# Joint attentions of a streaming encoder step: the next tile's transposes ahead of the prompt scores in seven steps of eight

## The chip, the cores and the metric

The kernel runs on one core of a Trainium2 chip. The metric is the device time of one execution in microseconds. Its engines are named as in the profile: PE (TensorE, matrix products; PEld is its weight load), DVE (VectorE), ACT (ScalarE), POOL (GpSimd) and SP (SyncE, which issues the DMAs). Before the change three runs took 3592.12, 3593.35 and 3600.36 us, median 3593.35.

## The reference

One inference step of a two-layer encoder trunk, in float32. 1024 new frames of one stream (the prompt) and 16 new frames of each of 8 running streams (the decode part, with a cache of 2048 earlier frames) go through a layer with window attention (A) and differential attention (B), and a layer with forgetting attention (C), each followed by a dense SwiGLU. B and C are the two joint attentions of this case. Cut to what they compute:

```python
# B: pairs of heads share values; chunk mask
scores = einsum('bthed,bshed->bhets', q2, k2) * SCALE
p = softmax(where(chunk_mask, scores, NEG_INF))
attn = p[:, :, 0] - lam * p[:, :, 1]
out = einsum('bhts,bshd->bthd', attn, v)
# C: 16 heads; scores get the summed log forget values; causal mask
scores = einsum('bthd,bshd->bhts', q, k) * SCALE + cq - ck
p = softmax(where(kpos <= qpos, scores, NEG_INF))
out = einsum('bhts,bshd->bthd', p, v)
```

Both are computed for the prompt over itself and for the decode frames over cache and new frames. Besides the two outputs of the trunk the kernel returns the new keys, values and forget values.

## The kernel before, in words

The program is a row of stages: projection for A and B, window attention of the prompt and of the decode frames, joint attention B (names with jb_), merge and feed forward, projection for C, joint attention C (jc_), merge and feed forward. B and C run the same function, `joint_attention`, which computes the prompt's attention and the decode attention together, interleaved by hand in one instruction list for each engine. There is no scheduler: what is written first on an engine runs first, and engines meet in semaphores that count up.

The work goes in units u, 8 in jb and 16 in jc. A unit is one prompt head (64 columns of query and key) plus a share of the decode attention of one stream, of which u's scores are made at the unit's end and its softmax and values in the next unit, u+1. The last pass of the loop finishes the last decode part. A unit has 8 steps s, one for each tile of 128 prompt queries; n = 8u+s counts the steps. A tile t attends to t+1 tiles of keys, and the tiles are taken in the order 3, 4, 2, 5, 1, 6, 0, 7.

For one tile n the prompt's work goes through the engines like this:

- `score(n)` on PE (L1489 to L1491): scores of the tile, t+1 tiles of 128 keys wide, in split float32 (two products, 3 to 5 matmuls with the mask). Even tiles write the PSUM buffer scores_a, odd ones scores_b, so score(n) waits for exponential n-2 (`exp_done`).
- DVE takes the negated row maximum (L1774, neg_top).
- ACT takes the exponential into probs (L1694). It waits for the maximum, and until turn(n-2) has read the same probs buffer.
- DVE takes the reciprocal of the row sums (L1783, inv).
- `turn(n)` on PE (L1500): t+1 transposes of 128 x 128 of the probabilities, in groups of four tiles into a ring of two PSUM slots (turned). It waits for exponential n, and in `ring_slot` until ACT has copied out what stood in the slot two groups ago.
- ACT copies each group to probs_t in SBUF (L1659), which frees the slot.
- `attend(k)` on PE (L1517), once for each pair of tiles 2k and 2k+1, in the odd step behind: values times probabilities, into PSUM pv. It waits for the copies, for ACT's copy of the pair before (o_copied) and for both outputs of the pair before (out_done).
- ACT copies pv to o_turn (L1703); `turn_back(k)` on PE (L1529 in jb, L1532 in jc) turns it back, into the other half of the same PSUM bank; DVE scales it with inv into out (L1809; L1805 in every other head of jb, where it adds to the first head's).

On DVE one step n issues, in this order: at odd n the output of pair (n-3)/2, then the maximum of tile n+3, half of the key transposes of the decode part (L1828) that belong to the step, other decode work, the reciprocal of tile n, and the other half of the key transposes.

On ACT a step n issues exponential n+2, at even n the copy of pv, and then copy_prompt(n+1), with the decode part's copies (L1714, L1680) and exponentials (L1727) between them.

On PE a step n issues score(n+3), turn(n+1), and then what the step's number asks for: score_new (L1569 to L1575), turn_probs (L1589), attend at odd n, attend_sample (L1607), score_keys at s=7 (L1544, L1552), turn_back at even n, turn_output (L1615). PE's list starts with score(0), score(1), score(2), turn(0).

The ring of two slots is shared: the groups of turn, the decode scores of the new frames (one slot, s=5) and half of the decode key scores (two slots, s=7) take slots in turn. After s=7 the first turn of the next unit therefore waits for ACT's copies of the key scores.

SP loads keys and values of cache and prompt into double or single buffers and stores the outputs; its list and POOL's set-up are not touched.

Of the kernel before, what the change touches and what calls it, by code (L numbers as in the profile page):

```python
# [1151 lines left out]
def joint_attention(nc, name, groups, planes, k_first, v, v_cols, dv, q_sample, q_first, k_cache, v_cache, k_new, v_new,  # L1152
# [51 lines left out]
    def tile_at(n):  # L1204
        return order[n % S]
# [27 lines left out]
    with Stage(nc, name) as st:  # L1233
# [55 lines left out]
        def scores_of(n):  # L1289
            return scores_a[:] if n % 2 == 0 else scores_b[:]  # L1290
# [171 lines left out]
        def _(pe):  # L1462
            def ring_slot(key):
                r = seq[key]
                if r >= ring:
                    old = key_at[r - ring]
                    pe.wait_ge(emptied_sem[engine_of[old]], count[old])
                return turned[:, r % ring]
# [7 lines left out]
            def score(n):  # L1476
                if n >= steps:
                    return
                h, t = n // S, tile_at(n)
                e = h % 2  # L1480
                if n % S == 0:
                    pe.wait_ge(qk_loaded[e], 16 * n_qk_loads * (h // 2 + 1))
                if n >= 2:
                    pe.wait_ge(exp_done, n - 1)
                size = (t + 1) * P
                dst, query = scores_of(n), slice(t * P, (t + 1) * P)
                for a in range(0, size, 512):
                    b = min(a + 512, size)
                    pe.matmul(dst[:, a:b], q_hi[:, e, query], k_both[:, e, a:b], start=True, stop=False)  # L1489
                    pe.matmul(dst[:, a:b], q_lo[:, e, query], k_hi[:, e, a:b], start=False, stop=(b < size))  # L1490
                pe.matmul(dst[:, size - P:size], ident_b[:], mask[:], start=False, stop=True).then_inc(scores_done, 1)  # L1491

            def turn(n):
                if n >= steps:
                    return
                pe.wait_ge(exp_done, n + 1)
                for g, (a, b) in enumerate(group_of_step[n % S]):
                    slot = ring_slot(("p", n, g))
                    for x in range(a, b):
                        last = pe.transpose(slot[:, (x - a) * P:(x - a + 1) * P], probs[:, n % 2, x * P:(x + 1) * P], ident[:])  # L1500
                    last.then_inc(turn_done, 1)

            def attend(k):
                if not 0 <= k < pairs_p:
                    return
                h, t = 2 * k // S, tile_at(2 * k)
                if k % S == 0:
                    pe.wait_ge(v_loaded[h // 2 % 2], 16 * (h // 4 + 1))
                wait_emptied([("p", n, g) for n in (2 * k, 2 * k + 1) for g in range(len(group_of_step[n % S]))])
                if k >= 1:  # L1510
                    pe.wait_ge(o_copied, k)
                    pe.wait_ge(out_done, 2 * k)
                first = 0 if diff else h % 2 * dv
                for x in range(tile_at(2 * k + 1) + 1):
                    part = 0 if diff else x % 2 * dv
                    e = 0 if x <= t else 1
                    last = pe.matmul(pv[part:part + dv, e * P:2 * P], vp[:, h // 2 % 2, x, first:first + dv],  # L1517
                                     probs_t[:, k % 2, x, e:2, :].rearrange("p e q -> p (e q)"),
                                     start=(x < P // dv), stop=(x > tile_at(2 * k + 1) - P // dv), skip_group_check=True)
                last.then_inc(pv_done, 1)  # L1520
# [37 lines left out]
            def score_new(u):  # L1558
                if u == 0:
                    pe.wait_ge(setup, 14)  # L1560
                    if not diff:
                        pe.wait_ge(later_loaded, 80)
                pe.wait_ge(ktn_done, u + 1)
                pe.wait_ge(q_done, 2 * (u + 1))
                if not diff:
                    pe.wait_ge(bias_loaded[u % 2], 80 * (u // 2 + 1))
                slot = ring_slot(("sn", u))
                if not diff:
                    pe.matmul(slot[:, 0:FRAMES], ident[:], later[:], start=True, stop=False, skip_group_check=True)  # L1569
                    pe.matmul(slot[:, 0:FRAMES], select[Q:2 * Q], bias[Q:2 * Q, u % 2, bank:], start=False, stop=False,  # L1570
                              skip_group_check=True, tile_position=(Q, 0))
                for step in range(4):
                    for c in range(4):
                        hb = 4 * c + step
                        last = pe.matmul(slot[Q * c:Q * c + Q, 0:FRAMES], q_blocks[Q:2 * Q, hb // 2, hb % 2],  # L1575
                                         ktn[:, Q * hb:Q * hb + FRAMES], start=(diff and step == 0), stop=(step == 3),
                                         skip_group_check=True, tile_position=(Q, Q * c))
                last.then_inc(turn_done, 1)

            def turn_probs(u, gi):  # L1580
                a, b = PG[gi]
                pe.wait_ge(s_exp_done, 2 * u + (1 if b <= per * 2 else 2))
                pe.wait_ge(s_copied, 2 * (u + 1))
                if gi >= 2:
                    pe.wait_ge(pt_copied, len(PG) * u + (1, 3, 4)[gi - 2])
                for t in range(a, b):
                    m = P if t < tiles - 1 else FRAMES
                    c = (t - a) * P
                    last = pe.transpose(s_ps[0:m, bank_of[gi], c:c + P], s_probs[:, t * P:t * P + m], ident[:])  # L1589
                last.then_inc(pt_done, 1)  # L1590

            def attend_sample(u, part):
                pe.wait_ge(pt_copied, len(PG) * u + (2, 4)[part])
                if part == 0:
                    pe.wait_ge(s_copied, 2 * (u + 1))
                else:
                    pe.wait_ge(vnew_loaded, 16 * (u + 1))
                for t in ((range(0, 2 * per), range(2 * per, tiles))[part]):
                    new = t == tiles - 1
                    m = FRAMES if new else P  # L1600
                    if new:
                        pe.wait_ge(pt_copied, len(PG) * (u + 1))
                    elif t % per == 0:
                        pe.wait_ge(vc_loaded[t // per], 16 * (u + 1))
                    for j in range(4):
                        values = vn[:, j * P:(j + 1) * P] if new else vc[:, t // per, t % per, j * P:(j + 1) * P]
                        last = pe.matmul(o_ps[32 * j:32 * j + 32, :], s_probs_t[0:m, t, 32 * j:32 * j + 32], values,  # L1607
                                         start=(t == 0), stop=new, skip_group_check=True)
                if part == 1:
                    last.then_inc(s_pv_done, 1)  # L1610
# [11 lines left out]
            for u in range(U + 1):  # L1622
                for s in range(S):
                    n = S * u + s
                    score(n + 3)
                    turn(n + 1)
                    if u < U and s == 5:
                        score_new(u)
                    if 1 <= u <= U and s == 5:
                        for gi in probs_at[s]:  # L1630
                            turn_probs(u - 1, gi)
                    if n % 2 == 1:
                        attend((n - 1) // 2)
                    if 1 <= u <= U and s == 3:
                        for gi in probs_at[s]:
                            turn_probs(u - 1, gi)
                    if 1 <= u <= U and s == 5:
                        turn_probs(u - 1, 4)
                        attend_sample(u - 1, 1)
                    if u < U and s == 7:  # L1640
                        score_keys(u)
                    if n % 2 == 0:
                        turn_back((n - 2) // 2)
                    if 1 <= u <= U and s == 4:
                        attend_sample(u - 1, 0)
                        turn_probs(u - 1, 2)
                    if 1 <= u <= U and s == 6:
                        turn_output(u - 1)
# [1225 lines left out]
```

## Time and profile before

| what | value |
|---|---|
| median of three runs | 3593.35 us |
| profiled execution | 3596.04 us, its span 3594.3 us, mean granted TensorE clock 0.966 |
| instructions in the profile | 62088 |
| PE busy | 3327.7 us, 93% of the span |
| PE weight load busy | 2908.6 us, 81% |
| DVE busy | 1598.0 us, 44% |
| ACT busy | 1124.3 us, 31% |
| POOL busy | 254.9 us, 7% |
| DMA | 493.16 MB, mean 137 GB/s |

The span is the time from the first to the last instruction of the program; the execution's own time has 1.7 us more around it. The busy shares are averages over stages of different kinds. The joint attentions are the stretches from about 416 to 702 us (jb) and from about 2063 to 2598 us (jc); the feed-forward stages fill most of the rest. A busy time of PE is not PE at its peak, because matmuls overlap and their ends are modelled. In the order of time, a row is a run of instructions of one line: its start, its length to the end of the last one, and in brackets the idle time before it and who ended it. Since matmuls overlap, the next row may start before the length has passed.

### The profile page before, as it was taken

The page shows a single profiled execution, that of the slowest core. Times are in us where ns is not written, and L with a number is a line of the kernel's source. Part 1 is how long each engine was busy: PE and PEld are TensorE (multiplying, and loading weights), DVE is VectorE, ACT ScalarE, POOL GpSimd, SP SyncE. Part 2 cuts the span into 40 slices and gives each one's busy share as a digit, 9 for nine tenths or more (in the row PEclk, how much of TensorE's full clock was granted, in tenths as well). Part 3 has the DMA queues.
Part 4 walks back from the last instruction along what each step waited for, and adds up shares of the span by engine and source line. Part 5 has one row for each costly group of instructions (what it writes and reads, how often), then busy time and mean ns, then how long its engine had stood idle before and what let it go on. Part 6 is the DMA issues. An engine that isn't in the chain of part 4 may idle for free. (4 is left out here: it accounts for less than half of the span.)

```text
span 3594.3 us, 62088 instructions
## 1 busy us (share of the span) xinstructions
PE 3327.7 (93%) x24520; PEld 2908.6 (81%) x24520; DVE 1598.0 (44%) x2913; ACT 1124.3 (31%) x2343; POOL 254.9 (7%) x338
## 2 busy tenths in 40 slices
PE   7997699798999999998799889999798999999997
PEld 7886477587999999997689866767577999999996
DVE  5427477463333333335331167777543333333334
ACT  4215355443212112112322155556433211121111
POOL 2310000032000000003000000000022000000003
PEclk9998799899999999999899999999999999999999
DMA  5436499533111111112554399999543111111112
GB/s 172 125 125 189 148 373 333 178 138 117 35 35 58 35 47 35 35 47 71 153 167 145 104 348 357 341 335 342 197 172 117 35 35 48 45 47 35 35 38 97
DMA packets 398381, 493.16 MB, mean 137 GB/s; under 512 B 68464, under 2 KB 250256, under 8 KB 398032
## 3 DMA queue, kind: packets, MB, share of 16 engines
q1 hardware_dynamic: 398176, 490.35, 41.2%
q8 instruction: 138, 2.26, 0.3%
q14 instruction: 67, 0.55, 0.0%
HBM read 407.10 MB, written 84.10 MB: 137 GB/s over the span
## 5 line engine op out<-in xcount | busy, mean ns | idle before, releaser
L2561 DVE TENSOR_TENSOR f_gated<-f_gated,f_up 128x384 f32<-128x384 f32 x132 | 73.1, 554 | 734.9 <-ACT f_gated L2491 734.9
L2585 DVE TENSOR_TENSOR f_y<-f_y,f_down 128x512 f32<-128x512 f32 x396 | 269.7, 687 | 229.4 <-PE f_down L2680 229.3
L2667 PE MATMUL f_gate<-m_ht_hi,f_w_hi 128*128 128x384 f32 x1056 | 355.0, 336 | 12.1 <-DVE f_w_lo L2612 12.1
L2667 PE MATMUL f_gate<-m_ht_lo,f_w_hi 128*128 128x384 f32 x1056 | 354.4, 336 | 0.0
L2667 PE MATMUL f_gate<-m_ht_hi,f_w_lo 128*128 128x384 f32 x1056 | 354.4, 336 | 0.0
L2667 PE MATMUL f_up<-m_ht_hi,f_w_lo 128*128 128x384 f32 x1056 | 352.7, 334 | 0.0
L2667 PE MATMUL f_up<-m_ht_hi,f_w_hi 128*128 128x384 f32 x1056 | 352.7, 334 | 0.0
L2667 PE MATMUL f_up<-m_ht_lo,f_w_hi 128*128 128x384 f32 x1056 | 352.7, 334 | 0.0
L2680 PE MATMUL f_down<-f_wo_hi,f_act_hi 128*128 128x512 f32 x792 | 313.4, 396 | 10.6 <-DVE f_y L2585 9.3
L2680 PE MATMUL f_down<-f_wo_hi,f_act_lo 128*128 128x512 f32 x792 | 309.9, 391 | 0.0
L2680 PE MATMUL f_down<-f_wo_lo,f_act_hi 128*128 128x512 f32 x792 | 309.6, 391 | 0.0
L2491 ACT ACTIVATE f_gated<-f_gate 128x384 f32<-128x384 f32 x132 | 65.0, 493 | 684.5 <-PE f_up L2667 684.3
L2667 PEld LDWEIGHTS f_gate<-m_ht_hi,f_w_hi 128*128 128x128 f32 x1056 | 199.5, 189 | 13.6 <-issue 12.8
L2667 PEld LDWEIGHTS f_gate<-m_ht_lo,f_w_hi 128*128 128x128 f32 x1056 | 199.5, 189 | 0.8
L2667 PEld LDWEIGHTS f_gate<-m_ht_hi,f_w_lo 128*128 128x128 f32 x1056 | 199.4, 189 | 0.0
L2667 PEld LDWEIGHTS f_up<-m_ht_hi,f_w_hi 128*128 128x128 f32 x1056 | 198.2, 188 | 0.0
L2667 PEld LDWEIGHTS f_up<-m_ht_lo,f_w_hi 128*128 128x128 f32 x1056 | 198.2, 188 | 0.0
L2667 PEld LDWEIGHTS f_up<-m_ht_hi,f_w_lo 128*128 128x128 f32 x1056 | 198.2, 188 | 0.0
L2680 PEld LDWEIGHTS f_down<-f_wo_hi,f_act_hi 128*128 128x128 f32 x792 | 149.5, 189 | 52.7 <-DVE f_y L2585 19.0
L1828 DVE STREAM_TRANSPOSE jc_kc<-jc_kc 128x512 f32<-128x512 f32 x256 | 180.8, 706 | 14.2
L2680 PEld LDWEIGHTS f_down<-f_wo_hi,f_act_lo 128*128 128x128 f32 x792 | 149.2, 188 | 31.8
L2680 PEld LDWEIGHTS f_down<-f_wo_lo,f_act_hi 128*128 128x128 f32 x792 | 149.5, 189 | 29.9
(404 smaller groups left out, 6756.6 us busy)
## 6 DMA issues: line engine op xcount, KB each, us to landing
jc_kc<-in_cache_c_k SPq DMA_DIRECT2D x64, 1024.0 KB, 11.1
jc_vc<-in_cache_c_v SPq DMA_DIRECT2D x64, 1024.0 KB, 10.3
jb_kc<-in_cache_b_k SPq DMA_DIRECT2D x32, 1024.0 KB, 11.7
jb_vc<-in_cache_b_v SPq DMA_DIRECT2D x32, 1024.0 KB, 8.6
m_raw<-in_w_ffn_in SPq DMA_DIRECT2D x44, 512.0 KB
f_raw<-in_w_ffn_in SPq DMA_DIRECT2D x44, 512.0 KB
f_raw_o<-in_w_ffn_out SPq DMA_DIRECT2D x22, 1024.0 KB, 6.2
m_raw<-x SPq DMA_DIRECT2D x18, 512.0 KB, 4.1
```

The source lines that it names most:

```text
L1828: dve.transpose(kc[:, u % 2, t, :], kc[:, u % 2, t + 1, :]).then_inc(kt_done, 1)
L2491: act.activation(silu[:, b], gate[:, q, 0:gw], ACT.Silu).then_inc(silu_done, 1)
L2561: dve.tensor_tensor(prod[:, b], silu[:, b], up[:, q, 0:gw], ALU.mult).then_inc(prod_done, 1)
L2585: dve.tensor_tensor(part, part, down[:, half, :], ALU.add).then_inc(added, 1)
L2667: last = pe.matmul(acc[:, q, 0:gw], a[:, s, k, u, :], b[:, k, token], start=(k == 0 and j == 0), stop=(k == KT - 1 and j == 2))
L2680: last = pe.matmul(down[:, half, :], a[:, s, t * P:(t + 1) * P], b[:, s, half * 512:(half + 1) * 512], start=(n == 0), stop=(n == 5))
```

## The change

In PE's list the order of the first two parts of a step is exchanged in the steps s=1 to s=7 of every unit: turn(n+1) stands first and score(n+3) second. In s=0 the order is the old one. No other list changes.

```diff
             for u in range(U + 1):
                 for s in range(S):
                     n = S * u + s
-                    score(n + 3)
+                    if s == 0:
+                        score(n + 3)
                     turn(n + 1)
+                    if s > 0:
+                        score(n + 3)
                     if u < U and s == 5:
                         score_new(u)
```

The first place is PE's list around s=2 and s=3 of a unit in jc: turn is L1500, score is L1489 to L1491, turn_back is L1532 and attend is L1517; x6 and x2 are the number of transposes.

```order
-L1500 MATMUL jc_turned<-jc_ident,jc_probs 128x128 x6
 L1532 MATMUL jc_pv<-jc_halves,jc_o_turn 128x64 x2
+L1500 MATMUL jc_turned<-jc_ident,jc_probs 128x128 x2
 L1489 MATMUL jc_scores_a<-jc_k_both,jc_q_hi 128x128
 L1490 MATMUL jc_scores_a<-jc_k_hi,jc_q_lo 128x128
 L1491 MATMUL jc_scores_a<-jc_mask,jc_ident_b 128x128
-L1500 MATMUL jc_turned<-jc_ident,jc_probs 128x128 x2
 L1517 MATMUL jc_pv<-jc_probs_t,jc_vp 64x256 x3
 L1517 MATMUL jc_pv<-jc_probs_t,jc_vp 64x128 x3
```

The two transposes of s=3 move from behind the step's score to in front of it, so the score now stands directly ahead of attend; the six of s=2 have left their place behind that step's score for one ahead of it.

The second place is PE's list around s=6 and s=7 of a unit in jc, with the same names; L1615 is turn_output.

```order
-L1500 MATMUL jc_turned<-jc_ident,jc_probs 128x128 x8
 L1532 MATMUL jc_pv<-jc_halves,jc_o_turn 128x64 x2
 L1615 MATMUL jc_s_ps<-jc_ident,jc_o_rows 128x128
+L1500 MATMUL jc_turned<-jc_ident,jc_probs 128x128 x4
 L1489 MATMUL jc_scores_a<-jc_k_both,jc_q_hi 128x384
 L1490 MATMUL jc_scores_a<-jc_k_hi,jc_q_lo 128x384
 L1491 MATMUL jc_scores_a<-jc_mask,jc_ident_b 128x128
-L1500 MATMUL jc_turned<-jc_ident,jc_probs 128x128 x4
 L1517 MATMUL jc_pv<-jc_probs_t,jc_vp 64x256
 L1517 MATMUL jc_pv<-jc_probs_t,jc_vp 64x128 x7
```

The eight transposes of s=6 no longer stand between that step's score and turn_back, and the four of s=7 stand ahead of the score instead of ahead of attend.

## Rows read from the trace of the kernel before

**Rows 1.** Busy time by window: jb and jc without their first units.
```profile
470.00:680.00 210.00, 201.09 (x2953) 158.82 (x2967) 156.74 (x369) 121.72 (x299) 0.00 (x0) 1.00 0.85 301
2110.00:2570.00 460.00, 438.47 (x6729) 322.10 (x6725) 335.44 (x757) 274.50 (x674) 0.00 (x0) 1.00 0.95 332
```

**Rows 2.** PE's waits in jc, 2110 to 2570: total us, times, longest.
```profile
PE jc_pv L1532 <- ACT jc_o_turn L1703: 9.0, 15, 0.6
...
PE jc_pv L1517 <- DVE jc_out L1809: 3.6, 15, 0.3
```

**Rows 3.** PE in order of time, one jc unit from 2265: start, length, what.
```profile
2267.54 0.36 PE L1489 MATMUL jc_scores_a<-jc_k_both,jc_q_hi 128*128 128x256 f32 x1
...
2267.93 0.49 PE L1500 MATMUL jc_turned<-jc_ident,jc_probs 128*128 128x128 f32 x3
...
2270.65 0.82 PE L1500 MATMUL jc_turned<-jc_ident,jc_probs 128*128 128x128 f32 x6
2271.31 0.56 PE L1532 MATMUL jc_pv<-jc_halves,jc_o_turn 128*128 128x64 f32 x4
...
2272.74 1.27 PE L1517 MATMUL jc_pv<-jc_probs_t,jc_vp 128*64 128x256 f32 x12 [0.23 <-DVE jc_out L1809]
...
2275.88 0.93 PE L1500 MATMUL jc_turned<-jc_ident,jc_probs 128*128 128x128 f32 x7
2277.41 0.66 PE L1532 MATMUL jc_pv<-jc_halves,jc_o_turn 128*128 128x64 f32 x4 [0.60 <-ACT jc_o_turn L1703]
...
2287.04 1.04 PE L1500 MATMUL jc_turned<-jc_ident,jc_probs 128*128 128x128 f32 x8
2287.92 0.56 PE L1532 MATMUL jc_pv<-jc_halves,jc_o_turn 128*128 128x64 f32 x4
...
2289.39 1.30 PE L1517 MATMUL jc_pv<-jc_probs_t,jc_vp 128*64 128x256 f32 x16
```

**Rows 4.** DVE in order of time, the same jc unit.
```profile
2271.08 1.07 DVE L1774 TENSOR_REDUCE jc_neg_top<-jc_scores_b 128x1 f32<-128x896 f32 x1
...
2272.14 0.46 DVE L1809 TENSOR_SCALAR jc_out<-jc_pv,jc_inv 128x64 f32<-128x64 f32 x2
...
2287.24 0.82 DVE L1774 TENSOR_REDUCE jc_neg_top<-jc_scores_b 128x1 f32<-128x640 f32 x1 [0.52 <-PE jc_scores_b L1491]
...
2288.67 0.44 DVE L1809 TENSOR_SCALAR jc_out<-jc_pv,jc_inv 128x64 f32<-128x64 f32 x2
```

**Rows 5.** ACT in order of time, the same jc unit.
```profile
2266.99 0.77 ACT L1659 ACTIVATE jc_probs_t<-jc_turned 128x512 f32<-128x512 f32 x2 [0.43 <-PE jc_turned L1500]
```

**Rows 6.** PE in order of time, one jb unit from 557.
```profile
559.99 0.52 PE L1500 MATMUL jb_turned<-jb_ident,jb_probs 128*128 128x128 f32 x3 [0.20 <-ACT jb_probs_t L1659]
...
565.35 2.20 PE L1517 MATMUL jb_pv<-jb_probs_t,jb_vp 128*128 128x256 f32 x12 [0.16 <-DVE jb_out L1809]
...
569.26 0.93 PE L1500 MATMUL jb_turned<-jb_ident,jb_probs 128*128 128x128 f32 x7
...
570.46 1.96 PE L1607 MATMUL jb_s_ps<-jb_vc,jb_s_probs_t 128*32 128x128 f32 x64
...
574.46 2.14 PE L1517 MATMUL jb_pv<-jb_probs_t,jb_vp 128*128 128x256 f32 x14
...
582.02 2.23 PE L1517 MATMUL jb_pv<-jb_probs_t,jb_vp 128*128 128x256 f32 x16
```

**Rows 7.** ACT in order of time, the same jb unit.
```profile
559.25 0.77 ACT L1659 ACTIVATE jb_probs_t<-jb_turned 128x512 f32<-128x512 f32 x2 [0.41 <-PE jb_turned L1500]
```

**Rows 8.** DVE in order of time, the same jb unit.
```profile
563.53 1.09 DVE L1774 TENSOR_REDUCE jb_neg_top<-jb_scores_b 128x1 f32<-128x896 f32 x1 [0.33 <-PE jb_scores_b L1491]
...
564.61 0.59 DVE L1809 TENSOR_SCALAR jb_out<-jb_pv,jb_inv 128x128 f32<-128x128 f32 x2
...
573.23 0.57 DVE L1809 TENSOR_SCALAR jb_out<-jb_pv,jb_inv 128x128 f32<-128x128 f32 x2
...
581.31 0.57 DVE L1809 TENSOR_SCALAR jb_out<-jb_pv,jb_inv 128x128 f32<-128x128 f32 x2
```

## The prediction

> **What bounds the kernel now.** The first view is the busy time of the engines over the two joint attention stages, without their first units [rows 1]. In jb PE is busy 201.1 of 210 us, in jc 438.5 of 460, at a granted clock of 1.00 (the higher of its two levels, 2.4 GHz) in both. DVE and ACT are near or under three quarters, the DMA engines at 0.85 and 0.95. PE's own instructions fill these stages, so a change of PE's order alone can win or lose only the time in which PE waits. The second view, PE's waits in jc, shows how little that is [rows 2]: 15 waits of 0.6 us, one a unit, for the ACT copy that turn_back needs, 9.0 us together, and 15 of at most 0.3 us for the output that attend waits for, 3.6 us. The third view is the order of time on PE, DVE and ACT in one steady unit of each stage, for the waits and for what stands just short of becoming one [rows 3 to 8].
>
> I call the steps of a unit s0 to s7. Step s holds score(s+3) and turn(s+1). The order table gives the turns of s1 to s7 the sizes 3, 6, 2, 7, 1, 8, 4 tiles, one transpose a tile. Eight transposes take 0.88 us of PE (2287.04 to 2287.92), so 0.11 each; six take 0.66 [rows 3].
>
> **The change part by part.** No instruction is added or removed, and none changes its engine or shape. DVE, ACT and the DMA queues keep their order. In s1 to s7 PE's transposes go in front of three to five score matmuls. Score(n+3) overwrites the scores that exponential n+1 reads, and turn(n+1) reads what that exponential writes, so both wait for the same event and that wait merely changes its holder. Three things do change.
>
> First, turn has a second wait, for a ring slot that ACT must have copied out. Until now the score stood in front of it and covered it. In jb turn of s1 waits 0.20 us for that copy even so, and starts 0.74 us after the copies begin (559.25 to 559.99) [rows 6, 7]. In front, it holds up the score, and everything behind it in PE's queue: 0.39 us of score (2267.54 to 2267.93 in jc, the same shape) now follow the wait instead of passing under it. jb: +0.39 in s1. In jc the copies begin at 2266.99 [rows 5]; 0.74 later is 2267.73, and PE arrives at 2267.54: +0.19. For the other turns I take no such wait: the copies they need stand in ACT's list a step earlier, and in s3, where one could be late, attend waits longer for its output (below). Bound 0.2 each, as in jb's s1.
>
> Second, each score ends later by the transposes put in front of it, and behind a score hangs a chain: DVE takes the row maximum, then a reciprocal, in s6 a key transpose, then scales the previous pair's output, and attend of the next odd step waits for that output, since both use one bank. attend starts 0.14 us after the output's end (2272.14+0.46 to 2272.74) [rows 3, 4], the maximum 0.20 us after PE's last score (2287.24 against 2287.04).
> - jc, s3: score(5) was done at 2270.65, the maximum could have begun at 2270.85 and began at 2271.08 only because DVE was busy. Now 0.19 of s1 and 0.66 of six transposes come first: 2271.70, 0.62 later. attend already waits 0.23 there, so it moves by the whole 0.62.
> - jc, s7: eight transposes stand in front of score(9), 0.88. The output ended at 2289.11, so attend could have started at 2289.25 and did at 2289.39: 0.14 of slack, 0.74 of new wait.
> - jb, s3: the maximum at 563.53 waited for PE, so it has no slack: 0.39+0.66 = 1.05 late, and attend at 565.35, which waits for the output (564.61+0.59) already, moves by 1.05.
> - jb, s5: seven transposes, 0.77, on top of the 1.05. The output ended at 573.80, now 575.62; attend at 575.76 instead of 574.46: 1.30 late.
> - jb, s7: the output ended at 581.88, now 1.30+0.88 later, 584.06; attend at 584.20 instead of 582.02: 2.18 late for the unit [rows 6, 8].
> - jc, s5: between score(7) and attend stand more PE work than in jb (turn_back of four matmuls, the bias rows), and there is no wait there today: I take nothing, bound 0 to 0.3.
>
> Third, a gain. In s4 turn_back waits for ACT's copy of the attention output: seven transposes, 0.77 of work, and 1.53 from their start to turn_back (2275.88 to 2277.41). With the score between them, and the step starting 0.62 later, PE reaches turn_back as that copy ends: -0.76 at most, -0.72 taken. In jb the same place takes 1.20 (569.26 to 570.46) for nine transposes of 0.99: -0.2, already inside the 1.30 of s5, which follows the output and not PE.
>
> Sum of a steady unit: jc 0.62-0.72+0.74 = +0.64, jb +2.18. jc has 15 such units after its first (the 15 waits of rows 2 are theirs), jb 7: 9.6+15.3 = 24.9. In jb every other unit adds its output to the first half's and has one more small DVE operation; I take the walked one for both. The first unit of each stage has no decode work on PE and waits for loads and for DVE's key transposes, so it may lose nothing or as much as a steady one; half of that is 1.4. Together +26.3.
>
> What the new neighbours cost each other on PE is not shown. Eight transposes end 1.04 after their start, but turn_back behind them starts after 0.88 [rows 3]: 0.16 at the end is overlapped there. A new boundary may lose such an overlap or win one: 0.16 x 7 steps x 22 units = 25 either way. I take zero, the row that is nearest.
> The Trainium skill (TensorE: Matmul & The Clock Gate, "Step-by-step: what each phase is for") says that PE's queue pulls weight loads ahead of running matmuls, so neighbours should cost each other nothing. By that rule this term is zero and the sum +26.3; by the row's 0.16, lost each time, the sum would be +51. The row's overlap speaks for the rule, but not for the new order.
>
> The sum stands on the profiled execution, 3596.04 us (span 3594.3): 3622.3. That execution is 2.7 us above the median of 3593.35, so the forecast for the median is 3620. Nothing below 10.8 us either way (0.3%) can be told from no change.
>
> **The rivals.**
> Only the last step counts. If ACT's earlier copies and DVE's slack hide the lag in s3 and s5, what is left is s7, 22 x 0.8 = 17.6, against 15 x 0.76 = 11.4 won in jc's s4: +6, 3600. For it: jc's maximum of s3 is late because of DVE today, not of PE. Against it: jb's waits 0.33 for PE [rows 8].
> Faster. The order was right for ACT: turn_back's waits go (9.0 us in rows 2), jb's small waits too (0.20 and 0.16 a unit, 8 units, 3), and the output chain stays hidden. It decides if the outputs have more slack than 0.88 in s7. Time: 3593-12 = 3581. For it: ACT is busy 274.5 of 460 us only, and PE waits for it by name. Against it: the slack is 0.14 in jc and nothing in jb.
> Boundaries give back. 0.16 saved at most of the 154 boundaries, some 20, against 26: 3600.
> The clock. The new waits are small, 0.6 to 1.1 us, two or three a unit. Rows 1 show 1.00 with some 2 waits a unit in them. If the granted clock fell to the lower level, 1.2 GHz, for 3% of 670 us, PE's work there would take twice as long: 20 more, 3640.
> The Trainium skill (same page, "A second HAM failure mode: psum-queue depth-cycling") says that frequent short idle times between groups of matmuls can make the clock swing between its levels. By that rule the last rival would be the likely one; rows 1, with 1.00 beside the existing waits, do not show it, so it stays small.
>
> **How the numbers follow.** Forecast 0.74 (3608 to 3634 by its own bounds: first units 0 to 2.8, jc's s5 up to 4.5, a third of the boundary term, 8, either way), only the last step 0.10, boundaries 0.05, faster 0.06, clock 0.05. The two cases at 3600 are within 0.3%; adding the tails of the forecast, faster 0.08, same 0.14, slower 0.78. The range goes down to 3597, to take in the cases at 3600, and up to 3640 for the clock.
>
> **What would show it.** In the profile after: PE's wait for jc_o_turn (9.0 us) gone or under 2; PE's waits of attend (L1517) for jc_out grown from 3.6 to 15 or more, with two a unit, in s3 and s7; in jb a wait for the ring copy of about 0.7 in s1 and three waits a unit for jb_out. The maxima on DVE start later after the transposes, by 0.66 in s2 and 0.88 in s6. A steady unit of jc becomes 0.6 longer, one of jb 2.2. It is wrong if attend does not wait longer in s7, if PE's wait for jc_o_turn stays, or if the units of jc keep their length.

## The result, and the profile after

The changed kernel took 3613.34 us, the one before 3596.99 us beside it (medians). The ratio is 1.0047 [1.0035, 1.0059], which is 16.9 us slower (16.4 by the medians). One of the changed kernel's eight runs took 5525.58 us at a mean granted clock of 0.554, for a reason that the runs do not show; it is left out of the ratio, and no other run reported here was like it. The profiled execution took 3613.26 us (span 3611.5) against 3596.04, 17.2 more; the forecast was 26.3 more there, 3620 for the median, range 3597 to 3640. The direction and the mechanism came as forecast, the size at two thirds. The reason given for the one gain did not hold ("Third", below).

The first view is PE's waits after the change, in jc: total us, times, longest. They answer to [rows 2].

```profile
PE jc_pv L1517 <- DVE jc_out L1812: 21.4, 30, 0.9
PE jc_s_ps L1552 <- issue: 3.2, 3, 1.6
```

And in jb (470 to 690), first the kernel before, then the changed one, where L1805 has become L1808 and L1809 has become L1812:

```profile
PE jb_pv L1517 <- DVE jb_out L1805: 3.1, 7, 0.7
PE jb_pv L1517 <- DVE jb_out L1809: 1.0, 6, 0.2
```

```profile
PE jb_pv L1517 <- DVE jb_out L1808: 12.2, 12, 1.4
PE jb_pv L1517 <- DVE jb_out L1812: 7.1, 9, 1.2
PE jb_turned L1500 <- ACT jb_probs_t L1662: 3.1, 6, 0.5
```

The 9.0 us of turn_back for jc_o_turn have no row any more. In their place attend waits 30 times for the output, two times a unit, 21.4 us where it was 3.6. In jb attend waits 19.3 us for outputs where it was 4.1, and turn 0.5 us a time for the ring slot. The windows show where the time went: PE is busy for 0.90 of the window in jb instead of 0.96 and for 0.945 in jc instead of 0.953, with the clock as before [rows 1].

```profile
470.00:685.00 215.00, 193.09 (x2810) 154.21 (x2813) 155.44 (x362) 122.13 (x293) 0.00 (x0) 1.00 0.82 289
2130.00:2590.00 460.00, 434.61 (x6752) 326.49 (x6750) 337.25 (x766) 277.65 (x676) 0.00 (x0) 1.00 0.94 332
```

The granted clock stays at 1.00, the level of 2.4 GHz, in both windows, with two to four waits of 0.2 to 1.4 us in every unit. The Trainium skill (TensorE: Matmul & The Clock Gate, "A second HAM failure mode: psum-queue depth-cycling") tells of a kernel whose clock swings with short idle times between groups of matmuls; this trace does not show it.

PE in order of time in the jc unit that starts at 2285.02 (the one that answers to [rows 3] started at 2265.42, 19.60 earlier):

```profile
2287.34 0.52 PE L1500 MATMUL jc_turned<-jc_ident,jc_probs 128*128 128x128 f32 x3
2287.61 0.36 PE L1489 MATMUL jc_scores_a<-jc_k_both,jc_q_hi 128*128 128x256 f32 x1
...
2289.32 0.88 PE L1500 MATMUL jc_turned<-jc_ident,jc_probs 128*128 128x128 f32 x6
2289.95 0.48 PE L1489 MATMUL jc_scores_b<-jc_k_both,jc_q_hi 128*128 128x512 f32 x1
...
2292.81 1.27 PE L1517 MATMUL jc_pv<-jc_probs_t,jc_vp 128*64 128x256 f32 x12 [0.80 <-DVE jc_out L1812]
...
2294.93 0.93 PE L1500 MATMUL jc_turned<-jc_ident,jc_probs 128*128 128x128 f32 x7
2295.62 0.48 PE L1489 MATMUL jc_scores_b<-jc_k_both,jc_q_hi 128*128 128x512 f32 x1
...
2296.70 0.61 PE L1532 MATMUL jc_pv<-jc_halves,jc_o_turn 128*128 128x64 f32 x4
...
2309.36 1.27 PE L1517 MATMUL jc_pv<-jc_probs_t,jc_vp 128*64 128x256 f32 x16 [0.62 <-DVE jc_out L1812]
```

attend of s3 waits 0.80 instead of 0.23 and attend of s7 0.62 instead of nothing; turn_back of s4 (2296.70) stands right behind its score. DVE shows why attend waits [rows 4]:

```profile
2288.62 2.33 DVE L1849 TENSOR_REDUCE jc_s_neg<-jc_s_scores 128x1 f32<-128x1024 f32 x2
...
2291.13 1.09 DVE L1777 TENSOR_REDUCE jc_neg_top<-jc_scores_b 128x1 f32<-128x896 f32 x1
...
2292.20 0.46 DVE L1812 TENSOR_SCALAR jc_out<-jc_pv,jc_inv 128x64 f32<-128x64 f32 x2
...
2307.36 0.82 DVE L1777 TENSOR_REDUCE jc_neg_top<-jc_scores_b 128x1 f32<-128x640 f32 x1 [1.34 <-PE jc_scores_b L1491]
...
2308.17 0.69 DVE L1831 STREAM_TRANSPOSE jc_kc<-jc_kc 128x512 f32<-128x512 f32 x1
2308.78 0.43 DVE L1812 TENSOR_SCALAR jc_out<-jc_pv,jc_inv 128x64 f32<-128x64 f32 x2
```

The output of s3 ends at 2292.66 and attend starts 0.15 later. The maximum ahead of it stands, as before, behind the two large maxima of the decode part (2288.62), with no idle time between: DVE's work since s1 sets its time. The maximum of s6 (2307.36) waited for PE, and behind it the key transpose, the reciprocal and the output run without a gap. PE in a jb unit from 563.16 [rows 6]:

```profile
565.47 0.52 PE L1500 MATMUL jb_turned<-jb_ident,jb_probs 128*128 128x128 f32 x3 [0.51 <-ACT jb_probs_t L1662]
...
571.70 2.20 PE L1517 MATMUL jb_pv<-jb_probs_t,jb_vp 128*128 128x256 f32 x12 [1.16 <-DVE jb_out L1812]
...
581.05 2.22 PE L1517 MATMUL jb_pv<-jb_probs_t,jb_vp 128*128 128x256 f32 x14 [0.21 <-DVE jb_out L1812]
...
589.51 2.23 PE L1517 MATMUL jb_pv<-jb_probs_t,jb_vp 128*128 128x256 f32 x16 [0.99 <-DVE jb_out L1812]
```

Here all four waits of the forecast stand: the ring slot in s1, the output in s3, s5 and s7.

### The profile page after: what moved, and what is told of

Its sections match the earlier page's. It is cut to its first block and busy times, and to the rows that moved or that the text cites. A ratio compares the mean times of both kernels' runs of the same rounds, so it can differ in the third digit from the quotient of the medians.

```text
span 3611.5 us, 62088 instructions
## 1 busy us (share of the span) xinstructions
PE 3325.3 (92%) x24520; PEld 2915.8 (81%) x24520; DVE 1598.1 (44%) x2913; ACT 1129.5 (31%) x2343; POOL 254.5 (7%) x338
## 3 DMA queue, kind: packets, MB, share of 16 engines
q8 instruction: 138, 2.26, 0.3%
```

## The experiments

Within one kernel the units of jc in which nothing stalls have the same length to 0.04 us, so unit lengths show in which step a change acts. The time of a whole execution holds stalls besides, told of in the last section. The table is worked out from the traces: the start of an instruction group after the start of the first prompt score of its unit, median over the units after the first whole one; "unit" is the length of an undisturbed unit of jc, "key scores" the time from a unit's start to jb's key scores. The last two columns are the ratio to before that these lengths give (15 units of jc, 7 of jb, over 3597) and the measured one. jb has two kinds of unit (key scores at 27.18 and 26.52 in the kernel before), and its median falls between them; it can be 0.3 off where one unit stalls.

| kernel | jc: attend s3 | jc: turn_back s4 | jc: attend s7 | jc: unit | jb: attend s3 | jb: attend s7 | jb: key scores | by units | measured |
|---|---|---|---|---|---|---|---|---|---|
| before | 7.33 | 12.00 | 23.97 | 30.65 | 8.20 | 24.69 | 26.85 | | |
| changed | 7.79 | 11.68 | 24.32 | 30.99 | 8.80 | 26.49 | 28.65 | 1.0049 | 1.0047 [1.0035, 1.0059] |
| even steps | 7.73 | 11.62 | 24.22 | 30.89 | 8.79 | 26.35 | 28.51 | 1.0042 | 1.0031 [1.0022, 1.0040] |
| odd steps | 7.78 | 12.04 | 24.22 | 30.84 | 8.42 | 24.91 | 27.08 | 1.0012 | 1.0027 [1.0017, 1.0037] |
| s4 alone | 7.33 | 11.99 | 23.94 | 30.63 | 8.20 | 25.06 | 27.22 | 1.0006 | 0.9994 [0.9985, 1.0002] |
| s2 of jc alone | 7.73 | 11.63 | 23.48 | 30.17 | 8.20 | 24.69 | 26.85 | 0.9980 | 0.9976 [0.9965, 0.9987] |
| changed, outputs early | 7.73 | 11.62 | 23.62 | 30.64 | 8.49 | 25.21 | 27.37 | 1.0010 | 1.0002 [0.9993, 1.0011] |
| changed, key transpose late | 7.79 | 11.68 | 23.73 | 30.70 | 8.84 | 26.20 | 28.36 | 1.0031 | 1.0028 [1.0017, 1.0039] |
| before, ACT's copy early | 7.33 | 11.23 | 23.08 | 29.77 | 8.20 | 24.67 | 26.83 | 0.9963 | 0.9964 [0.9953, 0.9974] |
| the same, outputs early | 7.33 | 11.23 | 23.10 | 29.86 | 7.69 | 24.05 | 26.20 | 0.9954 | 0.9970 [0.9960, 0.9981] |
| the same, outputs early in jb alone | 7.33 | 11.23 | 23.08 | 29.77 | 7.70 | 24.05 | 26.19 | 0.9951 | 0.9970 [0.9957, 0.9983] |

In five of the ten rows the ratio by units lies outside the measured interval, by 0.0002 to 0.0006 (even steps, odd steps, s4 alone, and the last two). What a unit gains or loses is therefore only part of what an execution does.

**The even steps alone.**

```diff
-                    if s == 0:
+                    swapped = s in (2, 4, 6)
+                    if not swapped:
                         score(n + 3)
                     turn(n + 1)
-                    if s > 0:
+                    if swapped:
                         score(n + 3)
```

> The turn stands ahead of the score only in s2, s4 and s6; s1, s3, s5 and s7 have the old order. Theory (the score of an even step ends late by the transposes in front of it, its maximum delays the output, and attend of the next odd step waits for that output): nearly all of the loss stays, since s2, s4 and s6 are the steps ahead of an attend. jc about +0.3 a unit (s3 +0.43, s4 -0.9, s7 +0.7 or so), jb about +1.75 (s3 0.6, s5 0.3, s7 0.85), 15 x 0.3 + 7 x 1.75 + first units 1 = 18: ratio to before 1.0045, between 1.003 and 1.006. Rival A (the ring slot: turn of s1 waits for ACT's copy with nothing in front of it): without s1 the loss is mostly gone, ratio under 1.0015. Rival B (each exchanged step costs the same, by its new neighbours on PE): 3 of 7 steps, 3/7 of 16.9 us = 7.2, ratio 1.002.

Measured: 1.0031 [1.0022, 1.0040], at the low end of the theory's range and above both rivals' values; jc +0.24 a unit, jb +1.66. Without s1 the loss stays, so the ring slot does not carry it. By positions all of it stands in the attends of s3 and s7 (and in jb's s5).

**The odd steps alone.** The same edit with `swapped = s % 2 == 1`.

> The turn stands ahead of the score only in s1, s3, s5 and s7; s2, s4 and s6 have the old order. Theory: the outputs of s5 and s7 are no longer late, so what is left is s1: the wait for the ring slot (0.2 in jc, 0.5 in jb) and, since DVE goes without a gap from the maximum of s1 to the output of s3 in jc, up to 0.45 there. The wait of turn_back in jc's s4 stays as it was before the change (about 9 us), because s4 has the old order. jc 0 to +0.35 a unit, jb +0.2 to +0.35: 3 to 8 us, ratio to before 1.0015, between 1.000 and 1.0025. Rival A (the ring slot carries the loss): the whole loss stays, less the gain of s4: 16.9 + 10, ratio 1.005 or more. Rival B (each exchanged step costs the same): 4 of 7 steps, 9.7 us, ratio 1.0027.

Measured: 1.0027 [1.0017, 1.0037], somewhat over the range; the unit lengths give 1.0012, inside it. In jc's s3 attend is as late as with all seven exchanges. PE, then DVE, in a unit of this kernel from 2306.94:

```profile
2309.53 0.36 PE L1489 MATMUL jc_scores_a<-jc_k_both,jc_q_hi 128*128 128x256 f32 x1
...
2314.71 0.65 PE L1517 MATMUL jc_pv<-jc_probs_t,jc_vp 128*64 128x256 f32 x4 [0.38 <-DVE jc_out L1813]
```

```profile
2310.12 0.42 DVE L1778 TENSOR_REDUCE jc_neg_top<-jc_scores_a 128x1 f32<-128x256 f32 x1 [0.35 <-PE jc_scores_a L1491]
...
2310.54 2.34 DVE L1850 TENSOR_REDUCE jc_s_neg<-jc_s_scores 128x1 f32<-128x1024 f32 x2
...
2313.05 1.07 DVE L1778 TENSOR_REDUCE jc_neg_top<-jc_scores_b 128x1 f32<-128x896 f32 x1
...
2314.11 0.46 DVE L1813 TENSOR_SCALAR jc_out<-jc_pv,jc_inv 128x64 f32<-128x64 f32 x2
```

The score of s1 (2309.53) follows three transposes, its maximum ends that much later, and the decode part's maxima and that of s3's pair run behind it without idle time. So s1's exchange and s2's each delay this attend by 0.40 to 0.45 alone, and by 0.46 together: they do not add. The wait of turn_back in s4 stayed (12.04). What the runs took beyond the unit lengths, some 5 us, is not settled; in the profiled execution stalls made jc 3.8 us longer than before (17.9 against 14.1, last section). Rival B's 1.0027 agrees with the time but not with the positions: 0.45 lost by s3, 0.41 of it given back at turn_back, whose time did not move, and 0.2 lost by s7.

**s4 alone.** The same edit with `swapped = s == 4`.

> The turn stands ahead of the score only in s4, in both stages; the other steps have the old order. Theory (the exchange has one place where it pays: jc's s4, where turn_back waited 0.6 for ACT's copy and now finds it ready, and s5 of jc has no output that is waited for): jc -0.7 a unit, 15 x 0.7 = 10.5; jb's s5 loses a little, 7 x 0.2 = 1.4. Sum -9 us, ratio to before 0.9975, between 0.9965 and 0.999. Rival A (what turn_back no longer waits is waited at attend of s5 or s7): ratio 1.000, and the wait shows there. Rival B (each exchanged step costs the same, by its new neighbours on PE, 0.11 us each): 22 x 0.11 = 2.4 slower, ratio 1.0007.

Measured: 0.9994 [0.9985, 1.0002]; the theory's 0.9975 is out. turn_back's wait is gone from the list, and turn_back still starts at 11.99. PE, then ACT, in a jc unit from 2303.97:

```profile
2313.42 0.60 PE L1500 MATMUL jc_turned<-jc_ident,jc_probs 128*128 128x128 f32 x4
2314.36 0.55 PE L1500 MATMUL jc_turned<-jc_ident,jc_probs 128*128 128x128 f32 x3 [0.34 <-ACT jc_probs_t L1663]
...
2315.95 0.66 PE L1532 MATMUL jc_pv<-jc_halves,jc_o_turn 128*128 128x64 f32 x4
```

```profile
2310.66 1.15 ACT L1731 ACTIVATE jc_s_scores<-jc_s_scores,jc_s_neg 128x1024 f32<-128x1024 f32 x1
...
2313.92 0.38 ACT L1663 ACTIVATE jc_probs_t<-jc_turned 128x256 f32<-128x256 f32 x1
...
2315.48 0.42 ACT L1707 ACTIVATE jc_o_turn<-jc_pv 128x256 f32<-128x256 f32 x1
```

The turn that now goes first waits 0.34 for the ring slot that ACT copies out at 2313.92, and turn_back starts 0.05 after the copy of o_turn ends (2315.90). From 2310.66, the first row, to that point ACT works without idle time, so ACT's list sets turn_back's start; PE's order in s4 only moves the wait from one instruction to another. My theory of the gain in s4 falls with this, and Rival A stands in a form that I had not named: the wait is taken within the step.

**s2 of jc alone.** The same edit with `swapped = not diff and s == 2`; `diff` is true in jb.

> The turn stands ahead of the score only in s2 of jc; everything else, jb too, has the old order. It asks where the gain at jc's turn_back of s4 comes from, after the exchange of s4 alone gave none. Theory (ACT, not PE, sets that turn_back: ACT works without a gap from s2 to s4, and the six transposes of s2, done earlier, let it copy earlier and so reach o_turn earlier): s2 alone brings turn_back of s4 forward to about 11.6 to 11.7 us after the unit's start, against 12.00, although attend of s3 goes from 7.33 to about 7.7. A steady unit -0.2 to -0.4, with nothing late in s7: 15 x 0.3 = 4.5 us, ratio to before 0.9988, between 0.998 and 1.000. Rival A (both exchanges, s2 and s4, are needed): turn_back stays at 12.0 or comes 0.4 late with attend, ratio 1.000 to 1.002. Rival B (any exchange costs by its new neighbours): slower by 15 x 0.1, no change in turn_back.

Measured: 0.9976 [0.9965, 0.9987], a little better than expected. PE, then ACT, in a jc unit from 2291.83, and the row of the kernel before that answers to ACT's first (its unit starts at 2265.42):

```profile
2302.68 0.93 PE L1500 MATMUL jc_turned<-jc_ident,jc_probs 128*128 128x128 f32 x7
2303.45 0.56 PE L1532 MATMUL jc_pv<-jc_halves,jc_o_turn 128*128 128x64 f32 x4
```

```profile
2296.96 0.93 ACT L1663 ACTIVATE jc_probs_t<-jc_turned 128x512 f32<-128x512 f32 x2
...
2301.14 0.37 ACT L1663 ACTIVATE jc_probs_t<-jc_turned 128x256 f32<-128x256 f32 x1
...
2302.76 0.39 ACT L1707 ACTIVATE jc_o_turn<-jc_pv 128x256 f32<-128x256 f32 x1
```

```profile
2271.36 0.87 ACT L1659 ACTIVATE jc_probs_t<-jc_turned 128x512 f32<-128x512 f32 x2 [0.63 <-PE jc_turned L1500]
```

ACT's copy of o_turn starts 10.93 after the unit's start; in s4 alone it was 11.51. Six transposes done ahead of the score let ACT copy them earlier: 5.13 after the unit's start instead of 5.94, where ACT had waited 0.63 for them. All of its list from s2 to s4 then moves forward; PE then reaches turn_back with no wait although attend of s3 is 0.40 later. One exchange of the seven gains, and its gain is a later step's.

**ACT's copy early.** The kernel before, with one instruction moved on ACT in jc.

```diff
-                    if n % 2 == 0:
+                    if n % 2 == 0 and (diff or u == 0 or s != 4):
                         copy_output((n - 2) // 2)
...
+                    if not diff and u >= 1 and s == 3:
+                        copy_output((n - 1) // 2)
                     if u >= 1:
                         for gi in probs_at[s]:
                             copy_probs(act, u - 1, gi)
```

> PE's and DVE's lists as before the change. On ACT, in jc alone, the copy of pv to o_turn that belongs to s4 is issued in s3, ahead of the decode part's copies of probabilities (0, 1) instead of behind them and behind an exponential. Theory (turn_back of s4 waits 0.6 only because that copy stands late in ACT's list): the copy ends 1.0 us earlier, turn_back's wait goes, and attend_sample, which needs the copies that are now 0.4 later, still finds them: jc -0.6 a unit, 15 x 0.6 = 9 us, ratio to before 0.9975, between 0.9965 and 0.9985. Rival (attend_sample takes over the wait, since its copies are late): ratio 0.9995 to 1.000, with a wait on PE for jc_s_probs_t.

Measured: 0.9964 [0.9953, 0.9974], and 0.9967 [0.9955, 0.9978] when it ran again:

> The kernel with the move on ACT in jc alone once more, on the same chip as its extension, to set the two against each other. It should come out at 0.9964 of before again, between 0.995 and 0.9975, with a steady unit of jc of 29.77.

This beats both kernels: by the ratios 13 us under the one before and 30 under the changed one. PE, then ACT, in a jc unit from 2293.82:

```profile
2304.27 0.93 PE L1500 MATMUL jc_turned<-jc_ident,jc_probs 128*128 128x128 f32 x7
2305.04 0.56 PE L1532 MATMUL jc_pv<-jc_halves,jc_o_turn 128*128 128x64 f32 x4
```

```profile
2304.05 0.39 ACT L1703 ACTIVATE jc_o_turn<-jc_pv 128x256 f32<-128x256 f32 x1
2304.32 1.10 ACT L1680 ACTIVATE jc_s_probs_t<-jc_s_ps 128x512 f32<-128x512 f32 x2
```

o_turn is copied by 2304.44, before the transposes of s4 are done, and turn_back runs in their wake. The unit is 0.88 shorter for a wait of 0.60: turn_back now starts 0.77 after the seven transposes start, 0.16 before their end, and what follows it starts 0.49 after it instead of 0.59. The Trainium skill (TensorE: Matmul & The Clock Gate, "Step-by-step: what each phase is for") says that a matmul's drain is hidden under the next one's fill only while they follow each other directly; the 0.16 agrees, as far as an end that the profile models can show it.

**Outputs early, in the changed kernel.** On DVE:

```diff
-                    if n % 2 == 1:
-                        output((n - 3) // 2)
                     if 1 <= u <= U and s == 6:
                         scale_output(u - 1)
                     maximum(n + 3)
+                    if n % 2 == 0:
+                        output((n - 2) // 2)
```

> The changed kernel, all seven steps exchanged, but on DVE the two outputs of a pair stand right behind the maximum of the even step instead of at the start of the next odd step: ahead of the reciprocal and of the key transposes. PE's list is that of the changed kernel. Theory (the loss is attend waiting for these outputs, which come late because DVE's list is followed in order): the outputs come earlier by what stood between them and the maximum (a reciprocal in s2, key transposes and small operations in s4, a key transpose in s6), so the waits of attend in s7 of jc and in s5 and s7 of jb shrink by most of their length; jc -0.7 a unit, jb -1.2: 15 x 0.7 + 7 x 1.2 = 19, ratio to the changed kernel 0.995, to before 1.000, between 0.998 and 1.002. Rival A (the score itself is late: the maximum of the next tile, the exponential and the next turn wait for it, and the output only seems to be the last): the time stays, ratio to before 1.004 or more. Rival B (the early output waits on DVE for turn_back and holds back the reciprocal and the transposes): slower than the changed kernel.

Measured: 1.0002 [0.9993, 1.0011], 0.9955 of the changed kernel by the two ratios. PE's list is the changed one, so what it wins over the changed kernel, 0.35 a unit in jc and 1.28 in jb, comes from the place of the outputs in DVE's list alone. PE's waits in jc:

```profile
PE jc_pv L1517 <- DVE jc_out L1812: 11.2, 15, 0.8
PE jc_turned L1544 <- issue: 4.1, 14, 0.3
```

The 15 waits in s7 are gone; those of s3 stay, where only a reciprocal stood in between. A new row of 0.3 a unit stands at the key scores, put down to no releaser. They start 0.21 after DVE's copy of the decode output (out_t) ends, 2325.45 and 2325.66 in one unit, and by the code they wait for it. DVE's list up to that copy is as long as before, so PE, which comes earlier now, waits there: 0.70 was won in s7 and 0.35 given back.

In jb the early outputs do not undo the exchange. The kernel with early outputs and the old order on PE, at the end of this section, has its key scores 1.17 earlier (26.20 against 27.37); with the outputs in their old place the exchange costs 1.80 there. 0.79 of the 1.17 is lost by s3, where PE still waits 1.1 a unit for the output. There the output already stands directly behind the maximum, so what is left is that the score, and with it the maximum, comes late.

**Key transpose late, in the changed kernel.**

```diff
                     if n % 2 == 1:
                         output((n - 3) // 2)
+                    if s == 7 and 1 <= u < U:
+                        turn_keys(u, parts * per - 1)
...
-                    turns = turns_at(u, s)
+                    turns = turns_at(u, s) if s != 6 or u == 0 else []
```

> The changed kernel, all seven steps exchanged; on DVE the last key transpose of a unit (key tile 15, in s6 ahead of the reciprocal and the output) is issued in s7 right behind the output, in every unit but the first. Theory (in s6 and s7 the chain is maximum, key transpose, reciprocal, output, attend, and each piece of it counts because DVE follows its list): attend of s7 comes 0.5 to 0.65 earlier, as with the outputs right behind the maximum, where the unit had 0.7; the key scores wait for that key transpose afterwards by up to 0.3 a unit. jc -0.3 to -0.6 a unit, jb -0.3 to -0.6: 6 to 13 us, ratio to the changed kernel 0.9975, to before 1.002, between 1.0005 and 1.0035. Rival (the transpose lies in a gap of DVE and the output waits for the exponential, by way of the reciprocal): no change, ratio 1.004 or more.

Measured: 1.0028 [1.0017, 1.0039] of before, as expected. attend of s7 comes 0.59 earlier in jc (0.69 is the length of the transpose taken out of the chain) and, unit by unit, 0.58 in jb (the medians, which fall between its two kinds of unit, differ by 0.29). So PE's score, the maximum, the transpose and the output are one chain in s6 and s7. The key scores then wait 0.24 a unit, again 0.21 behind the copy of out_t and not, as expected, for the key transpose itself.

**Both remedies.** ACT's copy early with the outputs early in both stages, then in jb alone, on the kernel before.

> PE's list as before the change; ACT's copy moved as in the kernel with that move alone, and on DVE the outputs right behind the maximum of the even step, in both stages. Theory (the waits on PE of the kernel before are turn_back's 0.6 and attend's 0.23 a unit in jc and attend's 0.16 in jb): turn_back's goes; attend's in s3 of jc shrinks by less than 0.1, because what stood between maximum and output there is one reciprocal; jc -0.65 a unit, jb -0.1: 10.5 us, ratio to before 0.997, between 0.996 and 0.9985. Rival (an earlier output makes DVE wait for turn_back and delays its key transposes, for which the key scores wait): ratio 0.998 to 1.000, worse than the move on ACT alone.

> PE's list as before the change; the copy of o_turn moved on ACT in jc; the outputs right behind the maximum in jb alone (in jc, where they made DVE's last key transpose late, they stay in their place). Theory: jc as with the move on ACT alone, a steady unit 29.77; jb as with the early outputs, a steady unit without other stalls 30.56 against 31.57, since attend of s1, s3 and s7 no longer waits 0.2 to 0.4: 7 more, in all 15 x 0.88 + 7 x 1.0 = 20 us, ratio to before 0.9945, between 0.993 and 0.996, and about 0.998 of the kernel with the move on ACT alone. Rival (jb's gain is eaten by stalls at the key scores, as in the kernel with both early outputs): ratio 0.996 to 0.997.

Measured: 0.9970 [0.9960, 0.9981], as expected, and 0.9970 [0.9957, 0.9983] with jb alone, where 0.9945 was expected. In jc the early outputs cost 0.09 a unit: the output now waits 0.45 on DVE for turn_back, the copy of out_t ends 0.54 later in its unit, and the key scores follow it by 0.21 once more (2290.86 and 2291.07). In jb the units are 0.65 shorter to the key scores, and yet the seven together took 224.9 us, against 223.5 and 224.8 in the two profiled executions with ACT's move alone. The rows for PE's waits in jb of the second kernel:

```profile
PE jb_scores_b L1490 <- issue: 1.8, 1, 1.8
PE jb_turned L1552 <- issue: 1.7, 1, 1.7
PE jb_turned L1575 <- issue: 1.5, 1, 1.5
PE jb_s_ps L1552 <- issue: 1.4, 1, 1.4
```

These four come to 6.4 us; in the second execution with ACT's move alone the same four came to 3.1. The rival that stalls eat jb's gain agrees with the time; what the stalls are is taken up in the last section.

## Why the prediction was right, and where it was not

**Which side.** Right: the new waits of attend outweigh the wait of turn_back that goes. jc rose from 30.65 to 30.99 a unit, jb by 1.34 to 2.17, 1.9 in the mean of its seven. 15 x 0.34 + 7 x 1.9 = 18.4, within the interval of 12.6 to 21.2 us around the measured 16.9. What failed is the size of single terms and the reason of the gain, below. The 1.4 for first units was not tested by itself: jb's first unit took 36.5 to 38.9 us in the four executions that leave jb as it was. Nor does the forecast's lower bound follow from its terms: 1.4 and 8 under 3620 is 3611, not 3608.

The agreement of 18.4 with 16.9 is in part luck. In the pair of profiled executions the 17.2 us lie otherwise: 13.5 between jb's first score and its last key scores, 6.3 from there to jc's first score (3.5 of them behind the end of jb, where no list changed), and jc up to its last key scores was 2.0 shorter, because its stalls were 7.1 shorter. That jc loses is shown by its unit length, not by its time in this pair.

**First, the ring slot.** It waits as said: 0.51 in jb's s1 (0.74 behind the start of the copies, as walked), and 0.20 in jc's, whose turn starts 2.32 after the unit's start where the score had started at 2.12. It cost less than 0.39: attend of s1 came 0.21 and 0.27 later in undisturbed units of one kind in jb and not at all in the others, which no longer wait 0.18 for an output there. That no other turn would wait for its slot is true of the changed kernel and false as a rule: with s4 alone exchanged, the slot cost 0.34.

**Second, the output chain.** Right in every place, and the cause of the loss: the rows of PE and DVE show it, and the early outputs and the late key transpose take part of it away in s7 of both stages and in s5 of jb. The maxima started later, as the signs said, by 0.45 in jc's s2 (0.66 forecast) and by 0.52 in s6 (0.88, less the 0.32 gained in s4). Sizes: jc's s3 0.46 instead of 0.62, since the two delays that I added (0.19 of s1 and 0.66 of s2) meet on DVE, which has no idle time from the maximum of s1 to the output, and do not add. jc's s7 lost 0.67 after the gain of s4 (from 0.32 early to 0.35 late), 0.74 forecast. jb's s3 came 0.64 to 0.91 later in six of seven units instead of 1.05, which is the ring term over again. In five of them s5 came 1.10 to 1.28 later (1.30 forecast) and s7 1.99 to 2.18 (2.18), in the second (which had a stall of 0.7 before the change) and the last unit s7 only 1.34 and 1.42.

**Third, the gain.** The size was right (0.72 forecast, 0.78 from s3 to s4 in the table), the reason was not, so the size was luck. The step said that the score between turn and turn_back covers ACT's copy. s4 alone, which puts that score there, gained nothing (turn_back at 11.99 instead of 12.00); s2 alone gained it all (attend of s3 0.40 later, turn_back 0.37 earlier). ACT's list, full from s2 to s4, set the wait, and it moves when its input, the six transposes of s2, comes earlier. I had written that ACT keeps its order and reckoned as if it kept its times.

**The rivals.** Only the last step counts: no, s3 lost 0.46 and jb's s3 and s5 lost too. Faster: no; the slack of 0.14 in s7 did not hold. Boundaries give back: no; jc's unit is 0.30 under the walk, and s3, s4 and s7 together explain 0.29 of it (0.16, 0.06 and 0.07), so 0.01 is left for the boundary term that was taken as zero. Clock: not in the profiled execution, with 1.00 in both windows.

## What to carry to other kernels

Before moving an instruction on the busy engine, ask of each wait not only who is late but what that engine did until then: a wait on an engine with no idle time ahead of it goes away by putting its list in another order (here one copy, 13 us) or by giving that list its input earlier (here six transposes of s2, 9 us). Reordering the waiting engine at the wait itself only moved it (s4 alone). When two delays meet at an engine that is already full, take the larger, not the sum: 0.40 and 0.45 gave 0.46 here. And read from undisturbed units in which step a reordering acts, but judge it by whole executions: these also hold stalls of the same size as the effect, and a gain by units (0.9951) can come out smaller (0.9970).

## What was not expected of the hardware

A wait cost more than its idle time: 0.60 us idle, 0.88 us of unit.

And PE stalled with no releaser in the view of its waits (its rows say "issue"), 0.2 to 2.0 us a time, mostly at the key scores. In jc such stalls, taken as the time from the first key scores to the last beyond undisturbed units, made up 7.0 us in the changed kernel, 14.1 in the one before, 17.9 with the odd steps exchanged. Many have a fixed place: units 1, 4 and 8 of jc, counted from 0, have one at their key scores in every one of the twelve profiled executions, unit 11 in eleven of them.

The DMA records of the traces tell what ended them. Beside the queue that moves data the page lists one whose packets are of the kind "instruction": packets, MB, share of the 16 engines.

```profile
q8 instruction: 138, 2.26, 0.3%
```

These are packets of 16 KB (2.26 MB by 138); in jc one starts every 8.1 to 9.7 us, by the median of each kernel. Behind the first units of both stages the twelve traces hold 110 such stalls of 0.2 us or more, without the key scores' wait for out_t. Every one of the 110 ended 2.3 to 2.8 us after one of these packets had started. So they are, as far as times can show it, waits of PE for its own instructions. Why a packet starts in time in one kernel and late in another, the runs do not tell.
